# Gathering a tile's token rows by quarters and transposing them on VectorE, one tile ahead, in a hybrid decoder layer with experts

## What is computed

```
gates = ...                       # [tokens, 16], two nonzero entries in a row
h = silu(einsum('cd,edf->cef', x, w_gate)) * einsum('cd,edf->cef', x, w_up)
h = h * gates[:, :, None]
y = einsum('cef,efd->cd', h, w_down)       # D = 1024, expert width 512
x = layer_norm(ALPHA * x + y, ln2_g, ln2_b)
```

## Time and profile before

| | |
|---|---|
| median of three runs | 1026.58 us (1020.91, 1026.58, 1030.8) |
| profiled execution, its own time | 1020.71 us |
| its span in the profile | 1018.7 us |
| mean granted TensorE clock | 0.956 |
| TensorE busy in the span | 909.4 us (89%), 4802 matmuls |
| VectorE | 687.5 us (67%) |
| ScalarE | 561.0 us (55%) |
| GpSimd | 366.0 us (36%) |
| queue of SP's loads | 143.85 MB, 38.4% of the 16 DMA engines |
| queue of GpSimd's gathers and scatters | 25.69 MB, 10.6% |

### The profile page before, as it was taken

One profiled execution on the slowest core, in us unless ns is written; L12 is line 12 of the kernel. 1 busy time (PEld: TensorE's weight loads), 2 busy tenths in 40 slices (PEclk: granted clock), 3 DMA queues, 4 the chain that ended last, 5 costly groups with the idle time before them and its releaser, 6 DMA issues.

```text
span 1018.7 us, 15879 instructions
## 1 busy us (share of the span) xinstructions
PE 909.4 (89%) x4802; PEld 712.9 (70%) x4803; DVE 687.5 (67%) x1017; ACT 561.0 (55%) x804; POOL 366.0 (36%) x238
## 2 busy tenths in 40 slices
PE   6999999999897899999918999999999999999920
PEld 5877888644465567888717888888887888888710
DVE  4339888896999945737697748798888734314326
ACT  4256576787686665702334646777777634323323
POOL 0000089999999990000000212213323211111116
PEclk9999999999799999999959999999999999999965
DMA  8550111000000100433565889999999897433264
GB/s 232 128 144 21 42 42 63 1 1 1 1 2 1 43 1 22 156 124 148 234 249 207 294 285 313 405 382 404 399 388 405 305 352 226 125 65 99 41 198 173
DMA packets 63052, 171.15 MB, mean 168 GB/s; under 512 B 19200, under 2 KB 33536, under 8 KB 50688
## 3 DMA queue, kind: packets, MB, share of 16 engines
q1 hardware_dynamic: 55664, 143.85, 38.4%
q0 software_dynamic: 7056, 25.69, 10.6%
q10 hardware_dynamic: 288, 1.05, 0.3%
HBM read 141.74 MB, written 26.21 MB: 165 GB/s over the span
## 4 chain that ended last, share of the span: by engine, by line
PE 45%; DMA 10%; DVE 6%; ACT 2%; issue 2%; POOLq 0%; POOL 0%; ACTq 0%; DVEq 0%; SPq 0%
PE ps L459 13%; PE ps L461 12%; PE ps L460 12%; DMA raw<-in_w_gate 8%; PE ps L924 2%; PE ps L797 1%; DVE wlo L1708 1%; DVE sm L1549 1%; ACT whi L1215 1%; PE ps L764 1%; PE ps L960 1%; PE ps L848 1%; DMA acc_d<-ysb,idx_add 1%; PE ps L784 1%; DVE xa L1563 0%
## 5 line engine op out<-in xcount | busy, mean ns | idle before, releaser
L1708 DVE TENSOR_TENSOR wlo<-raw,whi 128x2048 fp32r<-128x2048 f32 x96 | 216.0, 2287 | 51.2 <-ACT whi L1215 51.1
L1215 ACT CAST whi<-raw 128x2048 fp32r<-128x2048 f32 x96 | 180.4, 1912 | 47.9 <-DMA raw<-in_w_gate 18.5
L459 PE MATMUL ps<-whi,xgT_hi 128*128 128x512 f32 x384 | 152.0, 396 | 5.4 <-DVE xgT_lo L1718 5.4
L461 PE MATMUL ps<-whi,xgT_lo 128*128 128x512 f32 x384 | 149.8, 390 | 0.0
L460 PE MATMUL ps<-wlo,xgT_hi 128*128 128x512 f32 x384 | 149.5, 389 | 0.0
L1803 POOL TENSOR_SCALAR tapped<-hpad,par 128x1024 f32<-128x1024 f32 x30 | 92.0, 3067 | 3.0
L459 PE MATMUL ps<-xT_hi,w_hi 128*128 128x512 f32 (+1 forms) x224 | 87.2, 389 | 4.7 <-DVE w_lo L1304 3.0
L459 PEld LDWEIGHTS ps<-whi,xgT_hi 128*128 128x128 f32 x384 | 72.3, 188 | 21.3 <-issue 5.6
L461 PE MATMUL ps<-xT_hi,w_lo 128*128 128x512 f32 (+1 forms) x224 | 86.3, 385 | 0.0
L460 PE MATMUL ps<-xT_lo,w_hi 128*128 128x512 f32 (+1 forms) x224 | 86.3, 385 | 0.0
L1881 POOL COPY idx_now<-slot_token 128x1 int32 (+1 forms) x24 | 7.7, 319 | 218.7 <-PE ps L924 218.7
(11 more groups left out here) (305 smaller groups left out, 1825.0 us busy)
## 6 DMA issues: line engine op xcount, KB each, us to landing
raw<-in_w_gate SPq DMA_DIRECT2D x32, 1024.0 KB
raw<-in_w_up SPq DMA_DIRECT2D x32, 1024.0 KB, 12.7
raw<-in_w_down SPq DMA_DIRECT2D x32, 1024.0 KB
w_raw<-in_w_in SPq DMA_DIRECT2D x14, 512.0 KB, 4.1
x_tok<-in_x SPq DMA_DIRECT2D x8, 512.0 KB, 7.4
wo_raw<-in_w_o SPq DMA_DIRECT2D x16, 256.0 KB, 3.0
x_res<-in_x SPq DMA_DIRECT2D x16, 256.0 KB, 3.4
x_d<-xa SPq DMA_DIRECT2D x4, 512.0 KB, 6.0
```

Of the source, the lines that this page charges most:

```text
L459: pe.matmul(out, l_hi, r_hi, start=start, stop=False)
L461: return pe.matmul(out, l_lo, r_hi, start=False, stop=stop)
L1215: act.copy(whi[:, n, :], raw[:, n, :]).then_inc(gu_hi if n < 4 else dn_hi, 1)
L1708: dve.tensor_tensor(wlo[:, n, :], raw[:, n, :], f32(whi[:, n, :]), ALU.subtract).then_inc(gu_lo if n < 4 else dn_lo, 1)
```

## The change

The gather of tile 0 and its transposes on TensorE stay. For each later tile the gather is four indirect DMAs of 128 rows of 1 KB: DMA `t4` brings, for tokens 32 `t4` to 32 `t4` + 31 of the tile, the four quarters of their rows, the q-th quarter to partitions 32q to 32q + 31. The row numbers for it, four times the token's row plus q, are made once in `idx4`, by four small matmuls with the constant `spread` and one VectorE instruction. A single VectorE instruction, `x_turned`, then transposes all 32x32 blocks of `xg` into the new tile `xr` in SBUF, which holds what `pair(2)` held. `xgT_hi` and `xgT_lo` are made from `xr`. `x_turned(t + 1)` stands at the head of VectorE's `tile(t)`, before lo parts 0 to 2 of the weights. `xr` lies on the last row tile of the first norm's output, so its first use waits for `acc_out`, and SP's final read of `acc_d` waits for the last transpose.

```diff
+        xr = at("xr", [P, KT, P], F32, R2 + 12)
+        idx4 = at("idx4", [P, 4, TILES + 1], I32, 77.25)
...
+        x1_quarters = x1_d.rearrange("r (q n) -> (r q) n", q=4)
...
+        def x_source(t):
+            return pair(2) if isinstance(t, int) and t == 0 else xr[:].rearrange("p k n -> p (k n)")
...
+            sp.wait_ge(xg_tr, last_t + 2)
             sp.wait_ge(y_out, last_t * 16 + 16)
...
-            pe.wait_ge(rconst, 4)
+            pe.wait_ge(rconst, 5)
...
-            def xgT(t):
-                pe.wait_ge(xg_in, t * 16 + 16)
+            pe.wait_ge(table_set, 2)
+            for t4 in range(4):
+                last = pe.matmul(ps[:, 6, P + 32 * t4:P + 32 * t4 + TILES + 1], spread[:, t4, :], spare_no,
+                                 start=True, stop=True)
+            last.then_inc(table_mm, 1)
+
+            def first_xgT():
+                pe.wait_ge(xg_in, 16)
...
-            xgT(1)
             hidT(0)
             def tile(t):
                 gate_up(t, loads(t))
-                xgT(t + 1)
                 down(t - 1, loads(t - 1))
                 hidT(t)
...
-                act.copy(xgT_hi[:].rearrange("p k n -> p (k n)"), pair(2)).then_inc(xgT_hi_s, 1)
+                act.copy(xgT_hi[:].rearrange("p k n -> p (k n)"), x_source(t)).then_inc(xgT_hi_s, 1)
...
             dve.tensor_tensor(slot_token[:], spare_no, filled, ALU.add).then_inc(table_set, 1)
+            dve.tensor_tensor(spare_no, spare_no, filled, ALU.add).then_inc(table_set, 1)
...
+            for q in range(4):
+                link(dve.memset(quarter_no[32 * q:32 * q + 32, :], float(q)))
+            dve.wait_ge(table_mm, 2)
+            dve.tensor_scalar(idx4[:], ps[:, 6, P:2 * P].rearrange("p (t n) -> p t n", t=4), 4.0,
+                              quarter_no[:], ALU.mult, ALU.add).then_inc(table_set, 1)
...
-                dve.tensor_tensor(xgT_lo[:].rearrange("p k n -> p (k n)"), pair(2),
+                dve.tensor_tensor(xgT_lo[:].rearrange("p k n -> p (k n)"), x_source(t),
                                   f32(xgT_hi[:]).rearrange("p k n -> p (k n)"), ALU.subtract).then_inc(xgT_lo_s, 1)
+            def x_turned(t):
+                dve.wait_ge(xg_in, t * 64 + 16)
+                if isinstance(t, int) and t == 1:
+                    dve.wait_ge(acc_out, 16 * NT)
+                else:
+                    dve.wait_ge(xgT_lo_s, t)
+                dve.transpose(xr[:].rearrange("p b (t j) -> p t b j", t=4), xg[:].rearrange("p (t i b) -> p t b i", t=4, b=KT)
+                              ).then_inc(xg_tr, 1)
...
             split_new(1, range(3))
+            x_turned(1)
             hidden(0)
...
             def tile(t):
+                x_turned(t + 1)
                 split_new(t + 1, range(3))
                 hidden(t)
...
+            pool.tensor_copy(spread[:].rearrange("p t (q j) -> p t q j", q=4),
+                             ident[:].rearrange("p (t j) -> p t j", t=4).unsqueeze(2).to_broadcast([P, 4, 4, 32])).then_inc(rconst, 1)
...
             def fetch(t):
                 pool.wait_ge(xg_tr, t)
-                pool.tensor_copy(idx_now[:], slot_token[:, bass.ds(t, 1)]).then_inc(idx_set, 1)
+                pool.tensor_copy(idx_now[:].unsqueeze(2), idx4[:, :, bass.ds(t, 1)]).then_inc(idx_set, 1)
...
-                pool.indirect_dma_start(xg[:], None, x1_d, bass.IndirectOffsetOnAxis(ap=idx_now[:], axis=0)
-                                        ).then_inc(xg_in, 16)
+                for t4 in range(4):
+                    pool.indirect_dma_start(xg[:, 256 * t4:256 * t4 + 256], None, x1_quarters,
+                                            bass.IndirectOffsetOnAxis(ap=idx_now[:, t4:t4 + 1], axis=0)).then_inc(xg_in, 16)
```

## The result

The changed kernel took 1.022 times as long as the one before, 95% interval 1.0155 to 1.0285: 1047.3 us (median of four runs, 1046.0 to 1053.8) against 1026.3 us. That is slower, and outside the predicted range of 1012 to 1038 us. Two more executions fell in a slower state, the profiled one of 1070.5 us among them, so its rows show how a turn runs, and sizes are taken from the experiments. One of the experiments, called the probe kernel here, is the changed program unaltered up to 1042 us with a measurement behind it, and its rows are shown beside the others.

A forecast was written before the change was run, and what follows sets the result against it. TensorE was taken to bound the kernel, except in the loaded run, where weight loads set turns of 18.52 us. Loaded run +2.0 (early gain eaten), start +0.3, tail -7.9 sum to -5.6 us: 1021.0 us against median 1026.6, range 1012 to 1038.

The forecast's parts named there:

- Transpose on VectorE, 1.2 us: One added 32x32-block transpose of 128x1024 f32 a tile on VectorE, taken as 1.2 us; range kept 2.3.
- Rival 3: VectorE's transpose costs 2.3 us or more, making the loop 20.0 us and the kernel 1031 us; chance 0.10.
- To the issue 1.1 us: In the loaded run's gather loop, from VectorE's transpose to GpSimd's issue: 0.15 + 0.94 us, counted as 1.1.
- the issues "covered": GpSimd's four gather issues, 4 us and up to 9, fit in 9.7 us before the waiting scatter leaves.
- Drain of 36 packets a DMA engine, 12.3 us: Gather's packets in the loaded run: 36 pairs of 0.342 us, alternating with the other queue, 12.3 us.
- Rival 1: Gather drains four rows at a time, in about 4 to 5 us; loop under 17 us, kernel 1017 us; chance 0.27.
- Tail, 9 turns of 16.9 us: From 805 us on, TensorE loses 0.88 us of transposes a turn, nine times: 7.9 us gained.
- Loaded turns: In the run of fresh tiles, the transpose-gather loop sets turns of 18.9 us against 18.52 before, eight times.
- Rival 2: Gathered rows land later still, VectorE waiting before the lo parts in turns 6 to 14; 1047 us; chance 0.18.
- Start +0.3 us: Before VectorE's first lo part: six short instructions, 1.1 us, of which 0.76 was idle time; +0.3 us.
- early gain 3 us: Turns before the loaded run, mainly tiles 1 to 3, gain from TensorE's removed transposes: 3 us.
- the predicted -5.6 us: Whole kernel: +2.0 loaded run net of early gain, +0.3 start, -7.9 tail, sum -5.6 us.

The follow-up runs named there:

- plain transpose: Changed kernel with the block transpose reading its input in plain order instead of every eighth column (output not the layer's): 1020.6 us, 0.997 of the kernel before.
- useless transpose: Kernel before, TensorE's transposes and one gather kept, plus a block transpose on VectorE each tile whose result nobody reads: 1028.4 us, 1.005 of the kernel before.

## Why the prediction was wrong, step by step

- **Transpose on VectorE, 1.2 us: wrong, and the step that failed.** It took 2.15 us. I named the stride of 32 bytes as what would speak for 2.3, and still gave that case 0.10. With the price at 1.24 us and nothing else changed the kernel takes 1020.6 us.
- **Rival 3, 2.3 us gives 1031: right in what it named, mis-sized in what follows.** It reckoned 1.1 us a loop, eight times. Measured were 26 us between the two forms, since it had neither the full VectorE nor the index copy locked out through three lo parts.
- **To the issue 1.1 us, and the issues "covered": wrong.** With the transpose at 1.2 us it is 2.06 + 0.76 us to the first issue and 6.5 us to the start of the last (660.11 to 666.62), from which the landing counts. The prediction saw the slow copy and read it as load on GpSimd. It was VectorE's `wlo`, and the change moved the copy and four issues from behind TensorE's transposes to right in front of three of them.
- **Drain of 36 packets a DMA engine, 12.3 us: wrong.** The page's queue row of the changed kernel, and that of the kernel before:

```profile
q0 software_dynamic: 8208, 25.70, 10.3%
```

```profile
q0 software_dynamic: 7056, 25.69, 10.6%
```

  1152 more in 24 tiles is 48 a tile, not 432: four rows of 1 KB go as one packet. Rival 1's mechanism was right; the rule of packets of up to 4096 B stood in the Trainium skill, "DMA: Bandwidth & Descriptors", section "SWDGE vs HWDGE vs iDMA", the counts agree with it, and I gave it 0.27. In the loop of the 1.2 us transpose this error and the one on the issues nearly cancel, by luck: from the transpose's end 16.3 us to the landing where 17.7 were reckoned.
- **Tail, 9 turns of 16.9 us: right.** 16.83, and 7.3 us gained in the eight turns from tile 15 to 23.
- **Loaded turns: wrong.** 18.9 predicted, 18.4 to 25.9 measured.
- **Rival 2, rows later still, 1047: right in its sign, and in its time by luck, 0.18.** Its reason was the scatter's slow packets; the reason measured is the transpose's price and the locked-out issues.
- **Start +0.3 us and early gain 3 us: both wrong.** The rows are these: the start of the routing's `slot_col` matmuls on TensorE before and in the kernel with the plain transpose,

```profile
525.41 1.04 PE L918 MATMUL ps<-slot_col,slot_row 128*128 128x64 bf16 x16 [7.04 <-DVE slot_col L1653]
```

```profile
529.83 1.04 PE L928 MATMUL ps<-slot_col,slot_row 128*128 128x64 bf16 x16 [7.04 <-DVE slot_col L1667]
```

  and on VectorE the first `hid` behind it:

```profile
549.41 0.75 DVE L1725 SCALAR_TENSOR_TENSOR hid<-silu,slot_gate,ps 128x512 f32<-128x512 f32 x1 [4.78 <-ACT silu L1232]
```

```profile
556.41 1.25 DVE L1749 STREAM_TRANSPOSE xr<-xg 128x1024 f32<-128x1024 f32 x1 [6.67 <-DMA xg<-x_d,idx_now]
557.58 0.71 DVE L1756 SCALAR_TENSOR_TENSOR hid<-silu,slot_gate,ps 128x512 f32<-128x512 f32 x1
```

  24.0 us and 27.8 (28.2 in the probe kernel): the first transpose, which waits for four gathers, now stands in front of the first `hid`, +3.8 us where +0.3 was reckoned. From `hid` of tile 0 to that of tile 7 it is 123.9 us before and 124.2 with the plain transpose, so there is no early gain. From the `slot_col` matmuls to the end of the span it is 493.3 us before and 487.7 with the plain transpose: the predicted -5.6 us come out in these two traces by luck, as +3.8, +0.3 up to tile 15, -7.4 to tile 23 and -2.3 behind it. (The ratio of all runs says -3.2.)

## What to carry to other kernels

Before work moves to another engine, take the price of the exact operand pattern, strides too: here 0.9 us an instruction decided between a small gain and a loss of 2%. GpSimd's copies and gather issues should not fall under a run of VectorE instructions with two SBUF inputs; where they must, a second buffer takes most of the delay out (22 us lost became 5.5). An engine with 0.6 us left in a turn may still do (4.4 us lost with the useless transpose), as long as nothing that it waits for is late. And a transfer that a new wait puts in front of the first tile belongs in the sum.

## What the runs showed of the hardware that I had not expected

- VectorE's 32x32-block transpose of 128x1024 f32: 1.21 us with adjacent input elements, 1.98 us alone and 2.15 us in the kernel with elements 32 bytes apart, with either of the two outputs tried.
- GpSimd under VectorE: locked out by subtractions of two SBUF operands, by a plain f32 copy (5 GpSimd copies in 1.90 us) and by `tensor_scalar` (4 in 1.75; that both contend too stands in the Trainium skill, "SBUF — State Buffer", section "Who interferes with whom", and the trace agrees), and not by the block transpose (48 in 5.70) or a subtraction with a PSUM operand (30 in 3.40).
- An indirect DMA's issue is locked out as well: 1.01 us free, 2.27, 4.07 and 6.57 us under lo parts. A lock-out can last through three VectorE instructions in a row (a copy of 6.47 us).
- Gathers of 1 KB rows are packed four to a packet: 48 packets a tile more than with rows of 4 KB.
